# A layer boundary on one core: the first two weight panels behind it, one after the other or tile by tile together

## What is computed

```
h = h + 0.5 * rmsnorm(swiglu(rmsnorm(h, g_pre_ffn1), w_ffn1_gu, w_ffn1_down), g_post_ffn1)
mix = token_mixer(rmsnorm(h, g_pre_mix), ..., w_in, w_alpha_up, b_alpha, b_f, ...)
h = h + rmsnorm(mix, g_post_mix)
h = h + 0.5 * rmsnorm(swiglu(rmsnorm(h, g_pre_ffn2), w_ffn2_gu, w_ffn2_down), g_post_ffn2)
```

## Time and profile before

| | |
|---|---|
| median of 3 runs | 2059.01 us (2057.66 to 2059.4) |
| profiled execution | 2057.19 us |
| its span | 2055.3 us |
| PE busy | 1923.9 us, 94% |
| DVE busy | 1404.2 us, 68% |
| ACT busy | 908.6 us, 44% |
| mean granted TensorE clock | 0.958 |

### The profile page before, as it was taken

How to read it: one execution, slowest core, us unless ns; L and a number is a source line. 1 busy time by engine, 2 the same in 40 slices (tenths; PEclk the granted TensorE clock), 3 DMA queues, 4 the chain that set the end, 5 groups by cost and what they waited for, 6 DMA issues and landing times.

```text
span 2055.3 us, 36364 instructions
## 1 busy us (share of the span) xinstructions
PE 1923.9 (94%) x14822; PEld 1869.1 (91%) x14822; DVE 1404.2 (68%) x2171; ACT 908.6 (44%) x1347; POOL 100.4 (5%) x164
## 2 busy tenths in 40 slices
PE   7897889999799999999999999999999989999997
PEld 7896689988799989998999999999999889889997
DVE  6996576777766477745767777747774676677764
ACT  3443443444455444434555444434443455444442
POOL 0201031100000000002100000000000200000000
PEclk7998998989899999999999999999999999999999
DMA  9684110004355435543333535543554323353552
GB/s 354 254 307 142 42 62 1 1 1 163 106 185 206 180 128 181 187 155 122 103 110 117 172 136 174 186 173 128 179 187 158 130 90 124 112 196 128 187 199 102
DMA packets 41720, 301.42 MB, mean 147 GB/s; under 512 B 4544, under 2 KB 6736, under 8 KB 7808
## 3 DMA queue, kind: packets, MB, share of 16 engines
q1 hardware_dynamic: 41008, 296.90, 41.0%
q0 software_dynamic: 592, 2.87, 0.4%
HBM read 298.70 MB, written 1.05 MB: 146 GB/s over the span
## 4 chain that ended last, share of the span: by engine, by line
PE 76%; DVE 13%; DVEq 4%; ACT 3%; DMA 2%; issue 1%; POOL 0%; SPq 0%; ACTq 0%; POOLq 0%
PE acc L698 20%; PE acc L700 19%; PE acc L699 19%; DVE w_lo L669 3%; ACT w_hi L662 1%; PE mb L721 1%; PE acc L2052 1%; PE mb L2052 1%; DVEq L845 1%; DMA land<-in_w_in 1%; PE acc L2725 1%; DVE upd L794 1%; DMA ada_first<-in_w_ada 1%; DVE gla_sq L3063 1%; PE mb L2049 1%
## 5 line engine op out<-in xcount | busy, mean ns | idle before, releaser
L698 PE MATMUL acc<-h_hi,w_hi 128*128 128x272 f32 (+1 forms) x2960 | 871.6, 294 | 43.9 <-DVE w_lo L669 19.4
L700 PE MATMUL acc<-h_hi,w_lo 128*128 128x272 f32 (+1 forms) x2960 | 854.1, 289 | 0.0
L699 PE MATMUL acc<-h_lo,w_hi 128*128 128x272 f32 (+1 forms) x2960 | 852.7, 288 | 0.0
L669 DVE TENSOR_TENSOR w_lo<-land,w_hi 128x2048 fp32r<-128x2048 f32 (+1 forms) x239 | 576.1, 2411 | 169.4 <-ACT w_hi L662 168.8
L662 ACT ACTIVATE w_hi<-land 128x2048 fp32r<-128x2048 f32 (+1 forms) x239 | 479.3, 2006 | 479.2 <-PE acc L700 412.8
L698 PEld LDWEIGHTS acc<-h_hi,w_hi 128*128 128x128 f32 x2960 | 568.5, 192 | 57.5 <-DVE w_lo L669 23.2
L699 PEld LDWEIGHTS acc<-h_lo,w_hi 128*128 128x128 f32 x2960 | 568.3, 192 | 2.1 <-issue 0.2
L700 PEld LDWEIGHTS acc<-h_hi,w_lo 128*128 128x128 f32 x2960 | 568.4, 192 | 0.0
L698 PE MATMUL acc<-a_hi,w_hi 128*128 128x272 f32 (+1 forms) x880 | 251.8, 286 | 0.7 <-DVE w_lo L669 0.5
L699 PE MATMUL acc<-a_lo,w_hi 128*128 128x272 f32 (+1 forms) x880 | 250.3, 284 | 0.0
L700 PE MATMUL acc<-a_hi,w_lo 128*128 128x272 f32 (+1 forms) x880 | 250.2, 284 | 0.0
(11 more groups left out here) (555 smaller groups left out, 2561.4 us busy)
## 6 DMA issues: line engine op xcount, KB each, us to landing
land<-in_w_gu SPq DMA_DIRECT2D x110, 1024.0 KB, 4.8
land<-in_w_in SPq DMA_DIRECT2D x65, 1024.0 KB, 4.9
land<-in_w_down SPq DMA_DIRECT2D x40, 1408.0 KB, 6.0
ada_first<-in_w_ada SPq DMA_DIRECT2D x24, 1024.0 KB, 8.7
land<-in_w_ab SPq DMA_DIRECT2D x12, 1024.0 KB, 5.0
land<-in_w_out SPq DMA_DIRECT2D x12, 1024.0 KB, 4.8
land<-in_w_in_single SPq DMA_DIRECT2D x6, 512.0 KB, 3.5
const<-in_const POOLq DMA_DIRECT2D x1, 1134.0 KB, 11.1
```

The lines of the kernel that those rows point to most:

```text
L669: k.nc.vector.tensor_tensor(k.w_lo[:, p.par, 0:size * P], k.land[:, p.par, 0:size * P], k.w_hi[:, p.par, 0:size * P].bitcast(F32), ALU.sub ...
L698: mm(out, k.w_hi[:, par, c], hi, start=start, stop=False)
L699: mm(out, k.w_hi[:, par, c], lo, start=False, stop=False)
L700: return mm(out, k.w_lo[:, par, c], hi, start=False, stop=stop)
```

## The change

The first two panels behind each of the six boundaries are worked together: for each tile, PE waits for h_hi (`hh_ready`), does w_hi x h_hi and w_lo x h_hi for the four output tiles, then waits for h_lo and does w_hi x h_lo for the four. The third panel takes the weight buffer that the second, being in the third buffer, leaves free, and its products go to two banks of `mb`; from there on buffers (and one panel later accumulators) are counted one on. The fourth panel's split is written behind the copy-out of the first. In the input projection the three singles go: there are six doubles, with `small` as the first output tile, and one single, the seventh early panel; the decay work moves two panels back and its products to other banks.

```diff
-SINGLES, IN2 = 3, 19
-IN2_EARLY, MIXED = 5, 14
+IN2_DOUBLES, IN2_EARLY, MIXED = 6, 7, 14
+IN2 = IN2_EARLY + MIXED
...
+BOUNDARIES = tuple(M_LAYER + l * L_PANELS + first for l in range(LAYERS) for first in (L_GUA, L_IN, L_GUB))
...
     def of(cls, m, loop=0):
-        return cls(m // 2 + loop, m % 2)
+        weights_moved = sum(m >= first + 2 for first in BOUNDARIES)
+        banks_moved = sum(m >= first + 3 for first in BOUNDARIES)
+        return cls(m // 2 + loop, m % 2, (m + weights_moved) % 2, (m + banks_moved) % 2, m - 1 in BOUNDARIES,
+                   m - 2 in BOUNDARIES, 3 if m - 2 in BOUNDARIES or m - 3 in BOUNDARIES else 2)
...
+    def freed(self):
+        return self.count(3 - self.before)
...
+def out_banks(k, p, n, tiles=2):
+    return k.mb[:, 0:tiles, 0:n] if p.spare else k.acc[:, 2 * p.bank:2 * p.bank + tiles, 0:n]
...
 def split_hi(k, act, p, size):
...
-    act.wait_ge(k.panel_done, p.count(1))
...
+    if not p.third:
+        act.wait_ge(k.panel_done, p.freed())
...
 def panel_begin(k, pe, p):
     pe.wait_ge(k.lo_ready, p.count(3))
-    pe.wait_ge(k.acc_free, p.count(1))
+    pe.wait_ge(k.acc_free, p.freed())
...
-    p = Panel.of(start, loop)
-    panel_begin(k, pe, p)
+    two = [Panel.of(start + i) for i in range(2)]
+    for p in two:
+        panel_begin(k, pe, p)
     square_sum()
     for t in range(KT):
+        pe.wait_ge(k.hh_ready, (b + 1) * KT + (t + 1))
+        outs = [(p, out_bank(k, p, o, n), slice((o * KT + t) * P, (o * KT + t + 1) * P)) for p in two for o in range(2)]
+        for p, out, c in outs:
+            mm(out, weights_hi(k, p, c), k.h_hi[:, t, W], start=t == 0, stop=False)
+            mm(out, weights_lo(k, p, c), k.h_hi[:, t, W], start=False, stop=False)
         pe.wait_ge(k.hl_ready, (b + 1) * KT + (t + 1))
-        for o in range(tiles):
-            last = tile_mm(k, k.acc[:, 2 * p.par + o, 0:n], p.par, o * KT + t, k.h_hi[:, t, W], k.h_lo[:, t, W],
-                           t == 0, t == KT - 1)
-        if t == KT - 1:
-            last.then_inc(k.panel_done, 1)
+        for i, (p, out, c) in enumerate(outs):
+            last = mm(out, weights_hi(k, p, c), k.h_lo[:, t, W], start=False, stop=t == KT - 1)
+            if t == KT - 1 and i % 2 == 1:
+                last.then_inc(k.panel_done, 1)
         if t >= SUMS_BEHIND:
             square_sum()
...
-    p = Panel.of(start + 1, loop)
-    panel_begin(k, pe, p)
-    for o in range(tiles):
-        for t in range(KT):
-            last = tile_mm_third(k, k.acc[:, 2 * p.par + o, 0:n], o * KT + t, k.h_hi[:, t, W], k.h_lo[:, t, W],
-                                 t == 0, t == KT - 1)
-    last.then_inc(k.panel_done, 1)
-    pe_project(k, pe, start + 2, count - 2, tiles, W, loop)
+    for m in range(start + 2, start + min(count, 4)):
+        pe_project(k, pe, m, 1, 2, W)
+    if count > 4:
+        pe_project(k, pe, start + 4, count - 4, 2, W)
...
@@ act_gate_up_z, and the same with split_lo in dve_gate_up_z
-        if t > 0:
-            split_hi(k, act, p.ahead2(), GU_K if t < GU - 2 else nxt)
+        if t != 1:
+            split_hi(k, act, Panel.of(start + 3) if t == 0 else p.ahead2(), GU_K if t < GU - 2 else nxt)
...
@@ act_in_early (dve_in_early: split_lo in the same places, behind the copy-out)
+        if i != 1:
+            split_hi(k, act, Panel.of(start + 3) if i == 0 else Panel.of(start + i).ahead2(),
+                     early_sizes(3 if i == 0 else i + 2))
-        if i == 1:
+        if i == 3:
             act.wait_ge(k.dec_mm, l + 1)
...
-        elif i == 2:
+        elif i == 4:
             a(k.lf[0:8, :], k.lf[0:8, :], ACT.Exp, scale=-1.0)
...
@@ dve_in_early: undo_root at i == 0 -> 2, undo at 0 < i < 5 -> i > 2,
@@ minimum and memset at i == 2 -> 3, cumulative chain at i == 3 -> 5, scans and gst at i == 4 -> 6
...
@@ pool_mixer
-    pool.wait_ge(k.acc_free, Panel.of(M_LAYER + L_IN + 2, l * (L_PANELS // 2)).count(3))
+    pool.wait_ge(k.acc_free, Panel.of(M_LAYER + l * L_PANELS + L_IN + 4).count(3))
...
@@ program_tensor
-        pe_project_z(k, pe, l * 3 + 2, M_LAYER + L_SINGLE, SINGLES, 1, W2, loop)
-        pe_project(k, pe, M_LAYER + L_IN, 1, 2, W2, loop)
+        pe_project_z(k, pe, l * 3 + 2, base + L_IN, 3, W2)
         pe_gates2(k, pe, l)
-        pe_project(k, pe, M_LAYER + L_IN + 1, IN2_EARLY - 1, 2, W2, loop)
+        for i in range(3, IN2_EARLY):
+            pe_project(k, pe, base + L_IN + i, 1, early_sizes(i) // KT, W2)
```

More of the change, by code:

```diff
@@ L575, in load, with load_section @@
     sp.dma_start(k.land[:, par, 0:size * P], dram).then_inc(k.landed[par], 16)
-def load_section(k, sp, start, count, dram, size, loop=0):
+def load_section(k, sp, start, count, dram, size):
     def one(i, p, _):
@@ L582, in one @@
         load(k, sp, p.par, p.half, dram(i), size)
-    section(sp, start, count, one, loop)
+    section(sp, start, count, one)
 def ada_summed(n):
@@ L772, in pe_project @@
         peeled = 1
-    section(pe, start + peeled, count - peeled, one, loop)
+    section(pe, start + peeled, count - peeled, one)
 def dve_ada(k, dve, n, src):
@@ L930, in pe_branches @@
     if ready is not None:
-        one(None, Panel.of(start, loop), None)
+        one(None, Panel.of(start), None)
         peeled = 1
-    section(pe, start + peeled, count - peeled, one, loop)
+    section(pe, start + peeled, count - peeled, one)
 def pe_stat(k, pe, i, W):
@@ L1018, in pe_pre, with act_products @@
                            start=t == 0, stop=t == KT - 1).then_inc(k.sq_used, 1)
-def act_products(k, act, i, start, tiles, W, size, nxt, loop=0):
+def act_products(k, act, i, start, tiles, W, size, nxt):
     n = W.stop - W.start
@@ L1053, in one, with dve_post @@
         ahead(split_lo, k, dve, p, ahead_size, size)
-    section(dve, start, KT // tiles, one, loop, (nxt[0], None), unrolled=gain is not None)
-def dve_post(k, dve, i, W, gain, late=None, loop=0):
+    section(dve, start, KT // tiles, one, (nxt[0], None), unrolled=gain is not None)
+def dve_post(k, dve, i, W, gain, late=None):
     v = k.nc.vector
@@ L1112, in pe_stat_z, with act_products_z @@
     r.then_inc(k.stat_done, 1)
-def act_products_z(k, act, b, start, tiles, W, size, nxt, loop=0):
+def act_products_z(k, act, b, start, tiles, W, size, nxt):
     n = W.stop - W.start
@@ L1130, in one, with dve_products_z @@
             split_hi(k, act, p.ahead2(), nxt)
-            split_hi_third(k, act, Panel.of(start + count + 1, loop), nxt)
-    section(act, start, count, one, loop, ("next", None), unrolled=True)
-def dve_products_z(k, dve, b, start, tiles, W, size, gain, nxt, loop=0):
+            split_hi(k, act, Panel.of(start + count + 1), nxt)
+    section(act, start, count, one, ("next", None), unrolled=True)
+def dve_products_z(k, dve, b, start, tiles, W, size, gain, nxt):
     n = W.stop - W.start
@@ L1158, in one, with act_z @@
             split_lo(k, dve, p.ahead2(), nxt)
-            split_lo_third(k, dve, Panel.of(start + count + 1, loop), nxt)
-    section(dve, start, count, one, loop, ("next", None), unrolled=True)
+            split_lo(k, dve, Panel.of(start + count + 1), nxt)
+    section(dve, start, count, one, ("next", None), unrolled=True)
 SUMS_BEHIND = 2
 Z_GROUPS = ((0, 1), (1, 2), (2, 4), (4, 6), (6, 8))
-def act_z(k, act, b, post, W, gain, start, size, loop=0):
+def act_z(k, act, b, post, W, gain, start, size):
     a = k.nc.scalar.activation
@@ L1220, in dve_z @@
         rest(t)
-    split_lo(k, dve, Panel.of(start, loop).ahead2(), size)
+    split_lo(k, dve, Panel.of(start + 2), size)
 def dve_scale(k, dve, b, W):
@@ L1327, in one, with dve_gate_up @@
                                ACT.Copy).then_inc(k.ah_ready, 1)
-    section(act, start, GU, one, loop, nxt)
-def dve_gate_up(k, dve, i, start, W, nxt, loop=0):
+    section(act, start, GU, one, nxt)
+def dve_gate_up(k, dve, i, start, W, nxt):
     n = W.stop - W.start
@@ L1387, in pe_ffn, with act_copy_out @@
     else:
-        pe_stat_z(k, pe, pre, down, 1, W, loop)
-def act_ahead_only(k, act, start, count, size, nxt, loop=0):
-    section(act, start, count, lambda t, p, s: ahead(split_hi, k, act, p, s, size), loop, nxt, unrolled=True)
-def act_copy_out(k, act, start, count, tiles, dst, n, size, nxt, loop=0, signal=None):
+        pe_stat_z(k, pe, pre, down, 1, W)
+def act_copy_out(k, act, start, count, tiles, dst, n, size, nxt, signal=None):
     def one(i, p, ahead_size):
@@ L1447, in one, with act_merge @@
         dve.drain()
-    section(dve, start, AB, one, loop, nxt)
-def act_merge(k, act, i, start, n, W, nxt, loop=0):
+    section(dve, start, AB, one, nxt)
+def act_merge(k, act, i, start, n, W, nxt):
     def one(t, p, ahead_size):
@@ L1456, in one @@
                                ACT.Copy).then_inc(k.yh_ready, 2)
-    section(act, start, AB, one, loop, nxt)
+    section(act, start, AB, one, nxt)
 def tile(a, i, cols=slice(None), rows=slice(0, P)):
@@ L2542, in one @@
             a(k.e1[:, :, :], k.e1[:, :, :], ACT.Ln, bias=1.0).then_inc(k.dec_exp, 1)
```

(2 more changed lines are left out.)

323 lines of the change are left out of this document (158 added, 165 removed).

## The result

The changed kernel took 2039.12 us (median of 4, 2036.85 to 2041.18), the kernel before 2059.20 beside it: ratio 0.9908, 95% interval 0.9890 to 0.9926. The recorded ratio is not simply the quotient of the two medians; in the runs of this document the two lie up to 0.0012 apart, inside the interval. Forecast were 2050.0, range 2043 to 2058. It gained 20 us, twice the 9.1 that was forecast. The profiled executions stand at 2041.18 and 2057.19, 16.0 apart. I divide both into segments from one boundary's first statistics matmul to the next. Block 1, which is untouched, is 2.0 longer in the changed execution, with 122.9 us at a granted clock of 0.50 in place of 109.2; block 2 is 18.0 shorter.

What follows compares the result with a forecast made beforehand. TensorE was taken as the bound, with 76% of the chain. Likeliest gains of 1.7 + 1.35 + 0.65 + 0.65 + 2.8 + 1.9 = 9.1 us gave 2050.0 us as the median, range 2043 to 2058.

Steps and rivals of the forecast that it cites:

- Early start, gaps, A0: Layer 0's first gate-up: PE starts on h_hi and the pair fills gaps; gain 2.1 us, 1.7 after a stall.
- the pair's 15.75 us: Layer 0's first gate-up: the first two panels together are done 15.75 us after PE's start at full clock.
- the order of matmuls: First two panels: eight high-half then four h_lo matmuls over four banks keep 0.126 us each; change taken at 0.
- no idle from tile 2 on: Sign expected in the changed trace: in the first pair PE has no idle from tile 2 onward.
- Input projection at full clock: Input projection to first masked score: doubles replace three singles; gain 4.5 us in layer 0, 3.6 in layer 1.
- Wait at the entry: Mixer entry: the last single covers less of VectorE's chain; wait 5.7 us against 2.8, loss 2.7 per layer.
- Stall of 0.4 at the fifth gate-up panel: Gate-up, four times: the fifth panel's low half comes late; PE stalls 0.4 us, bounds 0 and 1.0.
- The clock: Boundaries: idle before the first tile untouched, so falls there stay; likeliest 3.4 us low at each input projection, others half way.
- B0 and B1: Second gate-up of each layer: gain -0.2 to 1.5 us each, 0.65 taken as likeliest.
- clock stays up: Rival: denser passes at the boundaries lose their low stretches; gain 15.0 us, time 2044.0; chance 0.15.
- Copy-out and weights lag: Rival: each gate-up section loses 1 to 1.5 us more before catching up; four times 1.3, 2055.2; chance 0.10.
- slower: Rival: the clock falls more, at passes over four banks and the longer mixer entry; 2062.6 us; chance 0.10.

Runs made afterwards that it cites:

- e3: Kernel before, plus idle matmuls (result unread) ahead of the first panel's waits and behind the first square sum at all six boundaries; ratio 0.9971 to before, 2050.52 us.
- e2: Changed kernel, still with the pair, but each tile waits for h_lo before its first matmul; ratio 0.9954 to the kernel before, 2044.69 us.
- e9: e2 (pair, late start) with the idle matmuls of e4 added; ratio 0.9924 to the kernel before, 2038.38 us.
- e6: Changed kernel, first two panels one after the other, the first starting each tile on h_hi; ratio 0.9959 to the kernel before, 2049.83 us.
- e10: e6 (one panel after the other, early start) with the idle matmuls of e4 added; ratio 0.9942 to the kernel before, 2044.31 us.
- e7: Changed kernel with the input projection's decay work one panel earlier; ratio 0.9873 to the kernel before, 2032.65 us.
- e4: Changed kernel plus idle matmuls, five ahead of the panels' waits, three or one behind the first square sum; ratio 0.9900 to the kernel before, 2036.21 us.

## Why the prediction missed

Three rungs at full clock separate the parts. At A0: before 208.6, one after the other with early start 208.1, pair 206.6. At I0, from e3: at most 62.5 (3.4 us of it low), then 60.3, then 58.8.

- **Early start, gaps, A0.** Forecast 1.7 (2.1 without the stall), measured 2.0. Right, as were the pair's 15.75 us, the order of matmuls at no cost, and "no idle from tile 2 on".
- **Input projection at full clock.** Forecast 4.5 and 3.6, measured 4.6 and 3.8. Wait at the entry forecast 5.7, measured 5.2.
- **Stall of 0.4 at the fifth gate-up panel.** None at A0, B0 and A1, and 0.3 at B1. The low half of that panel came just in time, since ACT began its high half at T + 7.9 and not T + 8.15 (T = 745.92); in the windows of the fourth panel and of the next PE has no idle:
```profile
755.72 2.29 DVE L700 TENSOR_TENSOR w_lo<-land,w_hi 128x2048 fp32r<-128x2048 f32 x1 [0.56 <-ACT w_hi L693]
```
```profile
752.00:758.00 6.00, 6.00 (x50) 6.00 (x49) 5.20 (x10) 3.30 (x5) 0.00 (x0) 1.00 0.52 175
758.00:764.00 6.00, 6.00 (x50) 6.00 (x49) 5.85 (x10) 2.67 (x3) 0.00 (x0) 1.00 0.53 178
```
- **The clock: the step that failed.** It said: "The first idle (statistics, root, first z) is not touched, so falls before the first tile stay", and took I0 and I1 with 3.4 us low each, A1 and B0 half way. At I0, B0, A1 and I1 the clock did not fall at all, in two profiles out of two. That idle was touched, by the prediction's own forecast: PE starts 0.75 us earlier, so that of the waits of 1.13 and 1.02 ahead of the first tile at I0 and A1 1.13 and 0.30 are left. e2 and e9 differ in idle matmuls alone, and so do e6 and e10; each time the low stretches go with them. So PE's idle time around the first tiles lets the clock fall, and more of it does so ahead of the first tile (e2) as well as between the first ones (e6). e10 fills it ahead of the first tile only and keeps the gap of 0.9 us between tiles, and the clock stays up: the two kinds make up for each other. The amount does not say by itself whether the clock falls: in e2 I0 fell and I1 did not with the same waits of 2.2 us, and B0 kept the clock in the changed kernel with 2.2 and lost it in e7 with 1.8. What else goes in stays open. At I0 and I1 that is 1.7 each of the 1.8 and 1.9 that the forecast fell short there (2.8 and 1.9 against 4.6 and 3.8). A1 gave 2.5 against 1.35.
- **B0 and B1: the term that was mis-sized.** 0.65 was given to each, bound 1.5. B0 gave 3.5, B1 0.6 (6.8 us low) to 1.9 (3.4), and would give 3.2 with none (e4). (B1 was taken to have B0's shape; its matmuls have 256 columns, not 272.) My own sums give 3.4 at full clock for B0 (1185.2 + 15.7 = 1200.9 against 1204.3), 3.0 with the stall, but I never worked out a B0 without any low stretch. Hence even the rival "clock stays up", the case that came true but for B1, stood at 15.0 and not at 18: 1.7 + 2.2 + 3.0 + 3.0 + 4.5 + 3.6 = 18.0, each gate-up term with its stall of 0.4. Measured in segments (mixers left out): 2.0 + 2.5 + 3.5 + 0.6 + 4.6 + 3.8 = 17.0, with B1 down; the two mixers add 1.0, which gives the 18.0 of block 2. In executions in which the old kernel falls at A0 too, 2.3 more.
- **The idle new at B0 and B1.** The first square sum now stands behind both panels' waits, also for the bank that the last copy-out frees. I had not seen it:
```profile
1179.58 0.70 PE L733 MATMUL mb<-sq,mean_ones 128*128 128x272 f32 x2 [1.46 <-DVE f L1161]
1180.98 0.40 PE L744 MATMUL acc<-h_hi,w_hi 128*128 128x272 f32 x1 [0.71 <-ACT h_hi L1192]
```
 It costs no time by itself, since h_hi is waited for behind it. At B1 the same wait is 1.92, and there the clock still falls in both profiles; e4 keeps it up with idle matmuls ahead of those waits. That this wait, by its length, is what makes B1 fall was not tried by itself; in e7 B0 fell with a wait of 1.13 there.
- **Ranges and chances.** The case "clock stays up" had a chance of 0.15. The Trainium skill ("TensorE: Matmul & The Clock Gate", "HAM oscillation — how this bites in real kernels") spoke for it, saying that waits between bursts of matmuls send the clock back and that denser work keeps it up. It had the direction right here, and e9 agrees with it: with the waits filled the clock stayed up, 0 us low at the six boundaries in place of 20.4. I held A1 against A0 against it, two shapes alike with different clocks. One profile could not carry that: in the second one of before A0 falls as well.
- **The other rivals.** "Copy-out and weights lag" did not come: behind the fifth panel of a gate-up section no stall is left that the kernel before has not too. Nor did "slower": over four banks the matmuls follow each other at 0.125 us with the clock at 1.00, and at or behind the mixer's entry, for all the longer wait, the clock is low for 6.8 us in layer 0 and 3.4 in layer 1, as it was before.

The profiled executions are 16.0 apart and the medians 20.1; both lie in the interval of the ratio (15 to 23 us). Block 1 is the same in all kernels, and ends (at the first statistics matmul of A0) between 720.4 and 728.1 us in the 13 profiles; in it the clock is low for 105.8 us in the shortest and for 126.3 in the longest. The 51 runs of the kernel before on three chips spread from 2046.19 to 2063.93, and the longer ones have the lower granted clock (0.954 for the two longest, 0.964 for the shortest). So a good part of the spread is low clock elsewhere in the program. The mixers, too, differ from one execution to the next of the same kernel (first score of layer 0 to the next statistics 184.2 and 187.3 us in the two profiles of the changed kernel).

## What to carry over

Where PE is the bound and its clock falls at a place, work out the case with no low stretch at all for every such place before giving it a share, and look at all of PE's idle around it, whether ahead of the first tile or between tiles. Two edits that bring nothing singly can bring much together: here the pair alone (e2) filled the gaps and paid 8.3 us for it at the lower clock, the early start alone (e6) left the gaps, and a low stretch costs most where the gaps have gone. Idle matmuls in the wait are a cheap test of whether the clock is at stake, before and after a change; here they were no gain that the total shows. A panel that is made smaller at the end of a stage takes its cover from whatever VectorE does behind it; move that work ahead in the same edit (5.5 us of earlier scores here).

## What the runs showed of the hardware

- A low stretch cost less than half its length where it lay among gaps: at A1 of the kernel before 3.4 us cost 0.5 (209.1 against 208.6 of e3), at B0 6.8 cost 1.2 (211.3, 210.1), and in e6 four of 3.4 cost 0.1 to 0.4 each against e10. Under the pair, without gaps, 3.4 cost 1.3 (B1 211.2 against 209.9, A1 of e2 against e9) to 1.5 (A0, I0 and B0 of e2 against e9) and 6.8 cost 2.6 (212.5 against 209.9), still below the 1.7 and 3.4 of half the length.
- In e2 0.7 us of added idle ahead of the first tile was enough for the granted clock to go from 1.00 to 0.50 (2.4 to 1.2 GHz) at four boundaries where the changed kernel kept it (one profile of e2; at I1 it stayed at 1.00).
- The clock at one place differs between executions of the same program: A0 of the kernel before was low for 0 us in one profile and for 6.8 in the other, B1 of the changed kernel for 6.8 and 3.4.
